# A weight slab's remainder in two halves between the levels of a recurrence, on GpSimd

## The reference

```python
diff = b[:, :, :, None, :] - b[:, :, None, :, :]
decay = jnp.exp(jnp.where(causal, diff, -jnp.inf))
attn = jnp.einsum('bhtk,bhtsk,bhsk->bhts', q_, decay, k_)
o = o_inter + jnp.einsum('bhts,bhsv->bhtv', attn, v_)
```

## Time and profile before

| | us |
|---|---|
| median of 3 runs | 1927.87 |
| lowest and highest | 1926.08, 1928.6 |
| the profiled execution | 1931.11 |
| its span | 1929.3 |
| mean granted TensorE clock in it | 0.947 |
| TensorE busy | 1763.0 |
| GpSimd busy | 704.2 |
| recurrence (TensorE's first product of head 0 to head 5's last output) | 655.4 to 792.6 |

### The profile page before, as it was taken

How to read it: one execution, slowest core, us unless ns; L and a number is a source line. 1 busy time by engine, 2 the same in 40 slices (tenths; PEclk the granted TensorE clock), 3 DMA queues, 4 the chain that set the end, 5 groups by cost and what they waited for, 6 DMA issues and landing times.

```text
span 1929.3 us, 24589 instructions
## 1 busy us (share of the span) xinstructions
PE 1763.0 (91%) x8605; PEld 1437.6 (75%) x8605; DVE 885.2 (46%) x1623; ACT 736.4 (38%) x1115; POOL 704.2 (36%) x362
## 2 busy tenths in 40 slices
PE   6999988998689898888999999989977989999999
PEld 4778845886678787766888888868855768888887
DVE  3585277446533255656444442253464554444200
ACT  4333266223344345413444442234423144454322
POOL 2344400343424565023444444533200334444444
PEclk9999999999789899788999999989987889999999
DMA  4233210232223211012333333322200123333333
GB/s 173 87 109 99 87 45 1 76 122 87 78 71 98 72 44 34 12 34 66 97 98 98 94 102 101 106 71 77 66 12 1 55 66 98 93 102 93 103 99 120
DMA packets 43275, 151.71 MB, mean 79 GB/s; under 512 B 4928, under 2 KB 5056, under 8 KB 43072
## 3 DMA queue, kind: packets, MB, share of 16 engines
q1 hardware_dynamic: 41184, 145.16, 24.2%
q10 hardware_dynamic: 2016, 5.53, 0.8%
HBM read 148.58 MB, written 2.10 MB: 78 GB/s over the span
## 4 chain that ended last, share of the span: by engine, by line
issue 57%; POOL 20%; PE 20%; ACT 1%; DVE 1%; DMA 1%; POOLq 0%; ACTq 0%; DVEq 0%
POOL WL L523 20%; PE DB L602 4%; PE DB L603 4%; PE DB L604 4%; PE SC L890 2%; PE DB L652 1%; PE DB L654 1%; PE DB L653 1%; PE OB L916 1%; DMA CONST<-in_consts_dram 1%; PE TB L671 0%; PE SC L892 0%; DVE TMP L1489 0%; PE SC L802 0%; POOLq L522 0%
## 5 line engine op out<-in xcount | busy, mean ns | idle before, releaser
L523 POOL TENSOR_TENSOR WL<-RAW,WH 128x1024 fp32r<-128x1024 f32 x268 | 648.0, 2419 | 1204.6 <-ACT WH L1087 1204.6
L1087 ACT ACTIVATE WH<-RAW 128x1024 fp32r<-128x1024 f32 x268 | 284.1, 1060 | 831.6 <-PE DB L604 369.2
L957 PE MATMUL DB<-XH,WH 128*128 128x512 f32 x704 | 277.6, 394 | 6.7 <-DVE XL L1493 6.6
L958 PE MATMUL DB<-XL,WH 128*128 128x512 f32 x704 | 275.7, 392 | 0.0
L959 PE MATMUL DB<-XH,WL 128*128 128x512 f32 x704 | 275.7, 392 | 0.0
L602 PE MATMUL DB<-XH,WH 128*128 128x512 f32 (+1 forms) x584 | 242.5, 415 | 14.4 <-DVE XL L1493 9.3
L603 PE MATMUL DB<-XL,WH 128*128 128x512 f32 (+1 forms) x584 | 230.7, 395 | 0.0
L604 PE MATMUL DB<-XH,WL 128*128 128x512 f32 (+1 forms) x584 | 230.3, 394 | 0.0
L957 PEld LDWEIGHTS DB<-XH,WH 128*128 128x128 f32 x704 | 133.0, 189 | 39.4 <-DVE XL L1493 7.8
L959 PEld LDWEIGHTS DB<-XH,WL 128*128 128x128 f32 x704 | 133.1, 189 | 28.0
L958 PEld LDWEIGHTS DB<-XL,WH 128*128 128x128 f32 x704 | 133.4, 189 | 26.9
(11 more groups left out here) (385 smaller groups left out, 2984.5 us busy)
## 6 DMA issues: line engine op xcount, KB each, us to landing
RAW<-in_stream_dram SPq DMA_DIRECT2D x268, 512.0 KB, 3.5
TP<-in_toep_dram ACTq DMA_DIRECT2D x4, 512.0 KB, 3.6
out_dram<-X SPq DMA_DIRECT2D x8, 256.0 KB, 4.1
X<-in_xt_dram SPq DMA_DIRECT2D x4, 256.0 KB, 4.9
X<-in_xt_dram ACTq DMA_DIRECT2D x4, 256.0 KB, 5.4
MRAW<-in_memt_dram ACTq DMA_DIRECT2D x1, 1024.0 KB, 5.6
CONST<-in_consts_dram ACTq DMA_DIRECT2D x1, 448.0 KB, 9.8
MSKI<-in_masks_dram ACTq DMA_DIRECT2D x1, 288.0 KB, 3.7
```

The source lines that it names most:

```text
L523: nc.gpsimd.tensor_tensor(WL[:, s, :], RAW[:, j, :], WH[:, s, :].bitcast(F32), ALU.subtract).then_inc(lo_done, 1)
L957: mm(o, WH[:, s, c], xh(k), start=(k == 0), stop=False)
L958: mm(o, WH[:, s, c], xl(k), start=False, stop=False)
L1087: A(WH[:, n % SPLIT, :], RAW[:, n % RING, :], ACT.Copy).then_inc(hi_done, 1)
```

## The change

`low_half` does half of a slab's remainder, 512 of 1024 columns; the first waits for the rounded slab, the second counts in `lo_done`. In the recurrence the loop behind the second level goes. Instead half 0 and 1 of the head's first slab follow the levels l = 1 and l = 2, and those of its second slab, in heads 1 and 2, l = 3 and l = 4.

```diff
+            def low_half(n, half):
+                j, s, c = n % RING, n % SPLIT, slice(SLAB // 2 * half, SLAB // 2 * half + SLAB // 2)
+                if half == 0:
+                    pool.wait_ge(hi_done, n + 1)
+                ins = nc.gpsimd.tensor_tensor(WL[:, s, c], RAW[:, j, c], WH[:, s, c].bitcast(F32), ALU.subtract)
+                if half:
+                    ins.then_inc(lo_done, 1)
...
-                    if l == 1:
-                        for n in slabs[h]:
-                            low((s0 + n) % RING, s0 + n)
+                    if 1 <= l <= 4:
+                        a, half = divmod(l - 1, 2)
+                        if a < len(slabs[h]):
+                            low_half(s0 + slabs[h][a], half)
```

## The result

The changed kernel is slower: 1939.2 us median (1938.8 to 1941.3, 4 runs) against 1928.2 (1926.1 to 1930.5, 4 runs), ratio 1.0061 with a 95% interval of 1.0046 to 1.0076. The forecast was 1935.8 in a range of 1931.0 to 1940.0. The profiled execution took 1939.07 us, its span is 1937.3. The page's busy shares hardly move: the time went into idleness and half speed.

A forecast was written before the change was run, and what follows sets the result against it. TensorE, busy 91% of the span and without slack in the recurrence, was taken as the bound. Stall 4.27, head 2 0.39 and clock 3.2 sum to +7.9 us, taking 1927.87 to 1935.8, range 1931.0 to 1940.0.

The forecast's parts named there:

- The stall: Head 1, first tile of hg1: waits for slab 3's second half, starts 4.27 us late, TensorE idle about 3.9.
- the half: GpSimd's half remainder: 1.16 us to the next start, 1.19 us to its own end.
- Nothing won back: Head 1: the third level comes 1.0 us sooner but gains zero, at most 1.0 us.
- Head 2: Head 2's first tile waits for slab 4's second half and starts 0.39 us late.
- The sixth level's thin cover: Head 2: later sixth level keeps 0.7 us of cover before its product; with halves of 1.53 some 0.4 us shows.
- Heads 3 to 5 and SyncE: Later levels there at most 1.2 us later, still covered; SyncE's later load of slab 6 harmless: zero cost.
- The clock in head 1: Behind head 1's idle stretch TensorE's clock falls to 0.50, 6.4 us at half speed, 3.2 us lost.
- Rival (a): Head 1's stall comes but the clock holds: 1932.6 us, chance 0.14.
- the sum: Whole kernel: 4.27 (head 1) + 0.39 (head 2) + 3.2 (clock) = +7.9 us, with no term for head 5.
- Rival (c): Not slower: head 5's low stretch shrinks from 13.2 to 6.4 us, returning 3.4; with Rival (a) 1929.2 us; chance 0.07.
- Rival (b): Head 1's low clock lasts as in head 5, 1939.2 us, or halves cost 1.53, 1937.8 us; chance 0.11.

The follow-up runs named there:

- the second comparison: Both kernels run again without edits: the kernel before 1926.99 us, ratio 0.9999; the changed kernel 1939.90 us, ratio 1.0062, 13.1 us over the before-median of 1926.8.
- all three with a small delay: Against the kernel before: halves in all heads but head 1, 0.9984; halves in head 2 only, 0.9977; whole remainders, slab 3's in head 1 behind the third level, 0.9986.

## Why the prediction was right or wrong

**Right in direction and in place.** The stall is where it was put, at the first tile of hg1: 4.52 us late by the matmuls' starts (0.41 at the hg0 tile and 4.11 more) for a forecast of 4.27, idle 3.96 for 3.9. What was mis-sized is the half: 1.27 us for 1.19 to its end, 1.22 for 1.16 to the next start, and TensorE saw it 0.15 later (682.56 to 682.71), not 0.05. From the third level's start to the hg1 tile that makes 682.71 - 675.23 = 7.48 us for 7.19, which covers the difference. I had divided the whole by two. Two halves take 2.54 us, one whole 2.34 (half of the pair's 4.68): an estimate from these is that 0.2 us of each instruction do not halve with its columns.

**Nothing won back.** All waits of TensorE in the kernel before are there after the change, at the same lengths, so the earlier third level was worth zero.

**Head 2:** 0.68 late for 0.39. Of this 0.55 is at the tile (half and hand-over, as in head 1) and 0.13 comes later in the head. There two instructions of VectorE and GpSimd meet and take longer, which I had not looked for; see the last section. The sixth level's thin cover held.

**Heads 3 to 5 and SyncE:** zero, and shown by themselves: halves in heads 3 to 5 alone give 1.0002. What I called zero in head 5 was right for the halves. They add nothing there.

**The clock in head 1:** it fell, 3.6 us lost for 3.2; 7.6 us of work were low, not head 0's 6.4. Rival (a), that the clock holds, is out: with slab 3's remainder behind the fourth level it fell even behind 1.8 us of idleness.

**The step that failed** is the sum's silence on head 5. It counted what the change does to TensorE's work where that is touched, and took the 13.2 us low of head 5 as a constant. They are not one. Changing when head 5 starts by 0.7 us makes them 6, by 8.8 makes them 25. Rival (c) named this mechanism and its place, and priced the one outcome, 6.4 us, as a gain of 3.4; that outcome exists (0.7 us of delay gives it, 24.5 us of head 5 become 21.1). The changed kernel got the other, a loss of 5.5, of which 0.8 returns in the attention behind. Rival (b) had a long low stretch, at the wrong head. With this term the count is 4.5 + 3.6 + 0.7 + 5.5 - 0.8 = 13.5 us, against 13.6 in the profiles, 13.1 by the second comparison's medians and 11.0 by the first's; the forecast was 7.9. That the time still fell inside the stated range is in part luck: the range reached up to 1940.0 because of a long low stretch in head 1, which did not come, and that room was filled by head 5's.

**Faster than both kernels** are all three with a small delay, best the one with halves in head 2 only, 0.9977 (0.9966 to 0.9988). The three intervals overlap. They save no work: their head 5 merely starts at a better moment, and a change elsewhere may take that back.

## What to carry to other kernels

Before a remainder, a copy or a load is spread between other steps, look up its first consumer: work that a saturated engine needs within the first step must not wait in line behind steps that wait for others. Where TensorE's clock falls behind idle stretches, a delay of a microsecond upstream can lengthen or shorten a low stretch far downstream by more than the delay; test such a change beside one that delays by the same amount in another way, and count from a common landmark rather than by spans. Here the halves in head 2 gained 0.2%, and whole remainders with one of them later gained 0.1%: such a gain belongs to the clock, not to the edit.

## What the runs showed of the hardware that was not expected

After 6.0 to 8.1 us of idleness, the same work of head 5 ran at half clock for 6, 13 to 14 or 22 to 25 us. Which of them it was went with the moment of its start, and it repeats from run to run well enough for several ratios to be clear of 1. Head 0, behind 7.6 us, had 6.4 to 6.6 us in thirteen of fourteen profiles.

A subtraction on GpSimd and a product on VectorE that met in the changed kernel's head 2 both ran longer. GpSimd's takes 0.61 us elsewhere in the head, VectorE's 0.72 in head 1 of the kernel before:

```profile
720.59 1.06 POOL L568 TENSOR_TENSOR SB<-HB 128x256 f32<-128x256 f32 x1
```

```profile
720.23 0.95 DVE L1762 TENSOR_TENSOR QX<-HKQ,SQ 128x512 f32<-128x512 f32 x1
```

The product reads both inputs from SBUF. It met two subtractions: one (from 720.00, 0.63 us) was running when it started, the other started under it. All six profiles of kernels with halves in head 2 have this meeting, with 0.95 to 0.98 us for the product and 1.06 for the second subtraction; in the other eight the two do not overlap there, and the product takes 0.71 to 0.72. VectorE's weighings, which read one input from PSUM, show no such cost: in the changed kernel 36 of 42 overlap a subtraction or a half, and they take as long as those that do not (0.67 to 0.69 us, and 0.80 to 0.84 for the seventh level's). The Trainium skill (SBUF — State Buffer, section SBUF: two separate sides) describes a port pair that VectorE, with two SBUF inputs, and GpSimd hold one at a time for a whole instruction. This trace agrees, with 0.45 us more for the subtraction and 0.23 more for the product.
